# The mixer of a two-block kernel: its work ordered by the layer norm's chain, and its last four input projections as plain fp32 products

## The reference, cut to what matters

```python
p = rmsnorm(h, g) @ w_in            # 1024 -> 1792 = 14 tiles of 128 features
p_pool, p_bval, p_bgate, p_cgate, p_cx = split(p)   # 2 + 2 + 2 + 4 + 4 tiles
# a: windows of 2, 4, 8, 16 tokens: mean - u, then 64x64 products, times a scale
# b: u = v*sigmoid(gate); depthwise conv of 31 taps; layernorm over 256; silu; @ w_pw
# c: conv of 4 taps; gates r, i = sigmoid(64x64 products); a = exp(-8 r softplus(-lam));
#    h = scan(a, sqrt(1-a*a) * i * xc); times gelu(c_gate)
h = h + concat(y_a, y_b, y_c) @ w_out    # 1024 -> 1024 = 8 tiles
```

## Time and profile before

| | |
|---|---|
| median of 3 runs | 1327.17 us (1326.48 to 1327.98) |
| the profiled execution: its own time | 1329.2 us |
| its span, first to last instruction | 1327.3 us |
| mean granted TensorE clock | 0.972 |
| PE busy | 1254.1 us (94%) |
| DVE busy | 846.9 us (64%) |
| ACT busy | 598.1 us (45%) |
| POOL busy | 70.9 us (5%) |
| the mixer's input projection starts | 785.9 us |
| its output projection starts | 909.5 us |

### The profile page before, as it was taken

One profiled execution on the slowest core, in us unless ns is written; L12 is line 12 of the kernel. 1 busy time (PEld: TensorE's weight loads), 2 busy tenths in 40 slices (PEclk: granted clock), 3 DMA queues, 4 the chain that ended last, 5 costly groups with the idle time before them and its releaser, 6 DMA issues.

```text
span 1327.3 us, 17556 instructions
## 1 busy us (share of the span) xinstructions
PE 1254.1 (94%) x6213; PEld 1026.9 (77%) x6213; DVE 846.9 (64%) x1196; ACT 598.1 (45%) x909; POOL 70.9 (5%) x58
## 2 busy tenths in 40 slices
PE   7899999999979999999997899867999999999997
PEld 6688888888867887777775689865888888888885
DVE  5978888888844356666667559996655422455222
ACT  6457656676633255555555542444332211222112
POOL 0011111011100000000000000121000000000000
PEclk9999999999989999999999799979999999999998
DMA  5333233332314332222221132111333333333332
GB/s 156 108 99 112 80 112 106 100 111 79 110 33 135 95 91 69 64 79 64 63 75 36 48 95 80 55 58 48 95 88 94 95 95 91 94 94 95 110 95 79
DMA packets 203289, 115.57 MB, mean 87 GB/s; under 512 B 3456, under 2 KB 201216, under 8 KB 202224
## 3 DMA queue, kind: packets, MB, share of 16 engines
q1 hardware_dynamic: 201472, 104.50, 27.5%
q0 software_dynamic: 1776, 10.53, 2.3%
HBM read 112.85 MB, written 2.16 MB: 87 GB/s over the span
## 4 chain that ended last, share of the span: by engine, by line
PE 78%; DVE 12%; ACT 5%; issue 4%; DMA 1%; SPq 0%; DVEq 0%; POOL 0%; ACTq 0%
PE psum L508 70%; DVE arena L1784 2%; DVE arena L1635 2%; ACT w_hi L919 2%; PE psum L693 1%; DVE w_lo L1344 1%; PE psum L586 1%; PE psum L594 1%; PE psum L577 1%; PE psum L517 1%; DMA w_raw<-a_w_in 1%; ACT L1116 1%; ACT arena L1116 1%; DVE stat L1639 1%; DVE arena L1647 1%
## 5 line engine op out<-in xcount | busy, mean ns | idle before, releaser
L919 ACT ACTIVATE w_hi<-w_raw 128x1024 fp32r<-128x1024 f32 x191 | 202.1, 1058 | 513.9 <-PE psum L508 512.5
L508 PE MATMUL psum<-a_hi,w_hi 128*128 128x512 f32 (+1 forms) x1000 | 361.3, 380 | 5.9 <-DVE w_lo L1344 5.9
L508 PE MATMUL psum<-a_lo,w_hi 128*128 128x512 f32 (+1 forms) x1000 | 355.8, 374 | 0.0
L508 PE MATMUL psum<-a_hi,w_lo 128*128 128x512 f32 (+1 forms) x1000 | 353.7, 372 | 0.0
L1344 DVE TENSOR_TENSOR w_lo<-w_raw,w_hi 128x1024 fp32r<-128x1024 f32 x191 | 234.3, 1227 | 158.6 <-ACT w_hi L919 158.2
L508 PE MATMUL psum<-b_hi,w_hi 128*128 128x512 f32 x640 | 257.6, 402 | 10.0 <-DVE b_lo L1523 4.1
L508 PE MATMUL psum<-b_lo,w_hi 128*128 128x512 f32 x640 | 256.1, 400 | 0.0
L508 PE MATMUL psum<-b_hi,w_lo 128*128 128x512 f32 x640 | 254.7, 398 | 0.0
L508 PEld LDWEIGHTS psum<-a_hi,w_hi 128*128 128x128 f32 x1000 | 183.7, 191 | 43.5 <-issue 7.2
L508 PEld LDWEIGHTS psum<-a_hi,w_lo 128*128 128x128 f32 x1000 | 183.0, 191 | 33.6
L508 PEld LDWEIGHTS psum<-a_lo,w_hi 128*128 128x128 f32 x1000 | 182.9, 191 | 31.9
(11 more groups left out here) (264 smaller groups left out, 1254.5 us busy)
## 6 DMA issues: line engine op xcount, KB each, us to landing
w_raw<-a_w_in SPq DMA_DIRECT2D x49, 512.0 KB, 3.8
w_raw<-w_up SPq DMA_DIRECT2D x32, 512.0 KB, 3.9
w_raw<-w_down SPq DMA_DIRECT2D x32, 512.0 KB, 3.7
arena<-acs POOLq DMA_DIRECT2D x8, 1024.0 KB, 5.0
w_raw<-a_w_out SPq DMA_DIRECT2D x16, 512.0 KB, 3.7
w_raw<-w_kv SPq DMA_DIRECT2D x16, 512.0 KB, 3.8
w_raw<-b_w_in SPq DMA_DIRECT2D x16, 512.0 KB, 3.8
w_raw<-w_in SPq DMA_DIRECT2D x14, 512.0 KB, 3.6
```

What stands on the lines that cost most here:

```text
L508: ins = mm(out, wv[:, u.par, k, :], xv[:, k0 + k, c0:c0 + cn], start=(first and begin and i == 0 and n == 0), stop=(last and end and i == ...
L919: ac(w_hi[:, u.par, :, :], w_raw[:, u.par, :, :], ACT.Copy).then_inc(S["hi_ready"], 1)
```

## The change

The weights of units 10 to 13 (c's gates) are no longer split. ACT multiplies them in place by the norm's gain, in 8 instructions of 128x128 (`whole`), and PE multiplies them in plain fp32 with h itself, for the 512 real tokens only (`in2_gate`). Since PE then reads w_raw, SP loads a later unit into that buffer only when the product is done. The order of the three engines is rewritten around b's layer norm: all long taps lie before it, ACT applies the norm, POOL's work goes to DVE, and the output projection's first two units start with b's and a's tiles.

```diff
-        pool_sums = (pls[:, 0, :], pls[:, 1, :])
+        pool_sums = ((pls[:, 0, :], pls[:, 1, :]), (cu[:, 0, 0:POOL_PAD + T2], cu[:, 1, 0:POOL_PAD + T2]))
-        lnt = place(NT, 2 * P, at=top[0] - 8 * T2)
+        lnt = dwo.rearrange("p a b -> p (a b)").rearrange("p (a b) -> p a b", a=NT)
--- SP
             for n, c in enumerate(IN2_TILES):
+                if n >= 12:
+                    sp.wait_ge(S["unit_done"], U_IN2 + n - 1)
                 load(Lin(U_IN2 + n), t["w_in_2"], 0, Lin(c * P))
+            sp.wait_ge(S["unit_done"], U_OUT2 - 1)
+            load(Lin(U_OUT2), t["w_out_2"], 0, Lin(0))
+            sp.wait_ge(S["unit_done"], U_OUT2)
+            load(Lin(U_OUT2 + 1), t["w_out_2"], 0, Lin(P))
--- POOL
...
-                steps.mark(add(a[:, 1:n], u[:, 1:n], u[:, 0:n - 1], ALU.add))
...
-                nc.gpsimd.tensor_tensor(xc[:, j, META:T2], xc[:, j, META:T2], cg[:, j, META:T2], ALU.mult).then_inc(S["yc_ready"], 1)
--- PE
+            def in2_gate(n, ks=range(KT)):
+                u, m = Lin(U_IN2 + n), Lin(M_IN2 + n)
+                if ks[0] == 0:
+                    pe.wait_ge(S["acc_read"], (m - 1).v)
+                    pe.wait_ge(S["hi_ready"], (u + 1).v)
+                for k in ks:
+                    ins = mm(bank(2 * m.par), w_raw[:, u.par, k, :], h[:, k, META:T2],
+                             start=(k == 0), stop=(k == KT - 1), skip_group_check=True)
+                if ks[-1] == KT - 1:
+                    ins.then_inc(S["unit_done"], 1)
...
+            in2(1, ks=range(4))
...
+            for n in range(2, 7):
+                in2(n)
+            gates(0)
+            in2(7)
+            gates(1)
+            in2(8)
+            in2(9)
+            gates(2)
+            in2_gate(10)
+            gates(3)
+            in2_gate(11)
+            in2_gate(12)
+            pe.wait_ge(S["dw_ready"], 2)
...
+            ins.then_inc(S["ln_tp"], 1)
+            in2_gate(13, range(4))
             pe.wait_ge(S["ln_ready"], 1)
...
+            in2_gate(13, range(4, KT))
             pe.wait_ge(S["cs_ready"], 2)
...
+            pe.wait_ge(S["pool_ready"], 2)
...
-            pe.wait_ge(S["yl_ready"], KT + 6)
-            out2(Lin(0), (4, 5, 6, 7, 0, 1), None, True, False)
-            out2(Lin(0), (2, 3), ("yl_ready", KT + 7), False, True)
-            out2(Lin(1))
+            out2(Lin(0), (2, 3, 0, 1), ("yl_ready", KT + 1), True, False)
+            out2(Lin(1), (2, 3, 0, 1), None, True, False)
+            out2(Lin(0), (4, 5, 6, 7), ("yl_ready", KT + 5), False, True)
+            out2(Lin(1), (4, 5, 6, 7), None, False, True)
--- ACT
+            def whole(u):
+                act.wait_ge(S[f"raw{u.par}"], (u.half * 16 + 16).v)
+                for k in range(KT):
+                    ins = ac(w_raw[:, u.par, k, :], w_raw[:, u.par, k, :], ACT.Copy, scale=gfm[:, k:k + 1])
+                ins.then_inc(S["hi_ready"], 1)
...
+            ac(bnst[:, 0, 0:1], one, ACT.Sigmoid)
...
+            def first_tap_long(j):
+                act.wait_ge(S["acc_read"], M_IN2 + 2 * j + 2)
+                at = C_DWW + DW_K * j + DW_K - 1
+                ac(dwo[:, j, :], cu[:, j, DW_K - 1 + META:DW_K - 1 + T2], ACT.Identity, scale=par[:, at:at + 1],
+                   bias=par[:, C_DWB + j:C_DWB + j + 1]).then_inc(S["tap0_ready"], 1)
+            for n in range(11):
+                if n in (0, 2):
                     act.wait_ge(S["acc_read"], M_IN2 + n + 1)
                     ac(bgt, bgt, ACT.Sigmoid).then_inc(S["bg_ready"], 1)
+                if 1 <= n < 8:
+                    hi(Lin(U_IN2 + n + 2))
+                if n >= 8:
+                    whole(Lin(U_IN2 + n + 2))
+                if n in (1, 3):
+                    first_tap_long(n // 2)
+                if 4 <= n < 8:
+                    first_tap_short(n - 4)
                 if n == 8:
                     gate_roots((0, 1))
...
+            whole(Lin(U_IN2 + 13))
+            act.wait_ge(S["ln_stat"], 1)
+            root(stat_at(N_SD), bnag[:, :, 1], eps2, 1.0, S["ln_sd"])
+            act.wait_ge(S["ln_shift"], 1)
+            for i in range(NT):
+                ins = ac(lnt[:, i, :], bank(1 + 2 * (i // 2))[:, 256 * (i % 2):256 * (i % 2) + 256],
+                         ACT.Identity, scale=stat_at(N_RS + i, 1), bias=stat_at(N_R2 + i, 1))
+            ins.then_inc(S["ln_ready"], 1)
+            gate_roots((2, 3))
+            hi(Lin(U_OUT2))
...   (silu of b, gelus(0), hi(U_OUT2+1), gelus(2), b_hi of b, of a, of c)
--- DVE
+            def whole(u):
+                dve.wait_ge(S["hi_ready"], (u + 1).v)
+                nc.vector.memset(bnag[:, 0, 0:1], 0.0).then_inc(S["lo_ready"], 1)
...   (first taps dropped, scans(j0) for two j interleaved, rnn_out(j) in place of POOL's,
...    window_means() for both tiles with 8 operations, evacuate(10..13) of 512 columns)
+            TAPS = {1: 2, 2: 5, 3: 3, 4: 1, 5: 1, 6: 1, 7: 1, 8: 8, 9: 10, 10: 16}
+            for n in range(11):
+                evacuate(n)
+                if 1 <= n < 8:
+                    lo(Lin(U_IN2 + n + 2))
+                if n >= 8:
+                    whole(Lin(U_IN2 + n + 2))
...
+            evacuate(11)
+            whole(Lin(U_IN2 + 13))
+            evacuate(12)
+            layer_norm_sums()
+            one_minus_a2(2)
+            one_minus_a2(3)
+            layer_norm_shift()
+            window_means()
+            lo(Lin(U_OUT2))
+            scans(2)
+            evacuate(13)
             lo(Lin(U_OUT2 + 1))
...   (b_lo of b, b_lo of a, rnn_out(0..3), b_lo of c)
-IN2_TILES = [2, 4, 3, 5, 10, 11, 12, 13, 0, 1, 6, 7, 8, 9]
+IN2_TILES = [4, 2, 5, 3, 10, 11, 12, 13, 0, 1, 6, 7, 8, 9]
```

More of the change, by code:

```diff
@@ new lines, in _ @@
+            pe.wait_ge(S["nrs_ready"], 2)
+            spread(bank(5), stat_at(N_RS), TOKENS1, S["nrb_ready"])
+            tp(bank(7)[:, 0:META], stat[0:META, N_R2 + 4:N_R2 + 5].to_broadcast([META, P]), ident[0:META, 0:META])
+            spread(bank(4), stat_at(N_R2), TOKENS1, S["nrb_ready"])
+            in2(1, ks=range(4, KT))
+            for n in range(2, 7):
+                in2(n)
+            pe.wait_ge(S["rr_ready"], 3)
+            gates(0)
+            in2(7)
+            gates(1)
+            in2(8)
@@ new lines, in _ @@
+            in2(9)
[5 more added lines that the diff above has]
+            pe.wait_ge(S["dw_ready"], 2)
+            pe.wait_ge(S["acc_read"], M_IN2 + 10)
+            for i, (c0, cn) in enumerate(TOKENS1):
+                for j in range(2):
+                    ins = tp(bank(1 + 2 * (i // 2))[:, 256 * (i % 2) + P * j:256 * (i % 2) + P * j + P],
+                             dwo[:, j, c0:c0 + cn], ident)
+            ins.then_inc(S["ln_tp"], 1)
@@ L1791, in short_conv @@
             def short_conv(j):
-                dve.wait_ge(S["acc_read"], M_IN2 + 5 + j)
                 c = xc[:, j, :]
-                w = [par[:, C_RGW + 4 * j + k:C_RGW + 4 * j + k + 1] for k in range(4)]
-                own(ts(c, cxp[:, 3:3 + T2], w[3], par[:, C_RGB + j:C_RGB + j + 1], ALU.mult, ALU.add))
                 for k in (2, 1, 0):
@@ L1845, in layer_norm_sums @@
                 for i in range(NT):
-                    own(nc.vector.bn_stats(bnst[:, i, :], psum[:, 4 + i // 2, 256 * (i % 2):256 * (i % 2) + 256]))
+                    own(nc.vector.bn_stats(bnst[:, i, :], bank(1 + 2 * (i // 2))[:, 256 * (i % 2):256 * (i % 2) + 256]))
                 own.wait()
@@ L1892, in _ @@
                     long_tap()
+                if n == 2:
+                    gated(1)
                 if n == 8:
-                    scan(0)
-                    scan(1)
-                if n == 10:
-                    means(0)
-                if n == 11:
-                    one_minus_a2(2)
-                    one_minus_a2(3)
-                if n == 12:
-                    layer_norm_sums()
-                    scan(2)
-                    layer_norm()
-            means(1)
-            lo(Lin(U_OUT2 + 1))
-            scan(3)
+                    scans(0)
+            evacuate(11)
[9 more added lines that the diff above has]
+            evacuate(13)
+            lo(Lin(U_OUT2 + 1))
+            for j in range(2):
+                dve.wait_ge(S["yh_ready"], KT + 1 + j)
+                tt(b_lo[:, 2 + j, 0:SEQ], bank(6 + j), f32(b_hi[:, 2 + j, 0:SEQ]), ALU.subtract).then_inc(S["yl_ready"], 1)
+            for j in range(2):
+                dve.wait_ge(S["yh_ready"], KT + 3 + j)
+                stt(b_lo[:, j, 0:SEQ], bank(4 + j), par[:, C_PSC + j:C_PSC + j + 1],
+                    f32(b_hi[:, j, 0:SEQ]), ALU.mult, ALU.subtract).then_inc(S["yl_ready"], 1)
+            for j in range(4):
+                rnn_out(j)
             rnn_low(0)
             rnn_low(1)
-            for j in range(2):
-                dve.wait_ge(S["yh_ready"], KT + 5 + j)
-                stt(b_lo[:, j, 0:SEQ], bank(2 + j), par[:, C_PSC + j:C_PSC + j + 1],
-                    f32(b_hi[:, j, 0:SEQ]), ALU.mult, ALU.subtract).then_inc(S["yl_ready"], 1)
```

(3 more changed lines are left out.)

222 lines of the change are left out of this document (107 added, 115 removed).

## The result

| | before | after |
|---|---|---|
| median | 1326.83 us (1325.66 to 1327.98, 4 runs) | 1313.68 us (1309.99 to 1315.17, 4 runs) |
| ratio of the two | | 0.9897, 95% interval 0.9874 to 0.9920 |
| span of the profiled execution | 1327.3 us | 1312.7 us |
| mean granted TensorE clock | 0.972 | 0.980 |
| third output unit starts | 922.2 us | 907.9 us |

13.2 us faster by the medians; the forecast was 1313.3. The span is 14.6 us shorter, and nearly all of it lies in the mixer: up to the mixer's first square sums both profiles agree to 0.1 us, and from the third output unit to the end they take 405.1 and 404.8 us. The page of the changed kernel answers to the earlier trace rows: VectorE has 12.7 us less to do, ScalarE 12.1 more, GpSimd 17.4 less.

What follows compares the result with a forecast made beforehand. TensorE bounds the whole span, but VectorE the changed stretch. Gains of 10.5 us before the norm, 3.4 to the output projection and 1.6 of clock, less one clock loss, gave -13.9: median 1313.3 us, range 1309.5 to 1319.5.

Steps and rivals of the forecast that it cites:

- VectorE's queue sets the stretch from 845.6 on: Mixer, 845.6 to the last long tap: VectorE's operations set the time, ending at 876.3 against 886.9, 10.5 us earlier.
- last tap, first turn: End of the long taps, for which TensorE's first turn of b waits: forecast at 876.3, before at 886.9.
- plain unit on TensorE: Gate units 10 to 13 in plain fp32: 0.855 us a block, 6.84 a unit, against 5.9 for a split one.
- third unit, clock lower once: Start of the third output unit: 906.75 at full clock instead of 922.2, with one clock loss of 1.6 us taken.
- GpSimd's hindrance: VectorE's slow rows beside GpSimd's window sums: with GpSimd's compute gone, 1.7 + 3.1 + 0.5 = 5.3 us come back.
- The scaling's cost: ScalarE's eight in-place scalings from 843.2, 2.4 us, release VectorE at 845.6; its split began at 844.2, so 1.4 us lost.
- The dearer products are hidden in this order: Units 10 to 13: TensorE pays 3.8 us more in all, hidden because it waits 2.3 us for the taps.
- The order: Norm's chain from the first turn to the output projection: 19.35 us instead of 22.6, counted as 3.4 us of gain.
- The lower clock once, at the output: First two output units: a saving of 1.6 us from the lower clock was open, so the loss was taken once.
- the swing of the clock through all short waits: Second rival: the clock falls in the short waits from 856 on; gain 12 to 13 us, 1314 to 1315; chance 0.15.
- The rival of plain products at the lower level: Third rival: plain fp32 products run at 1.71 us a block, 13.7 a unit; +10 us, 1337; chance 0.03.
- rival 1: Behind the long taps: a wait replaces their 10 us; gain only 7 to 11 us, 1316 to 1320; chance 0.18.

Runs made afterwards that it cites:

- e1: The changed kernel with units 10 to 13 split into fp32r halves again instead of plain fp32 products, same order; median 1314.04 us.
- e7: The kernel before without GpSimd's six window additions, so the pool branch lacks its sums; median 1322.21 us.
- e2: The changed kernel with five additions of 128x512 on GpSimd beside the long taps; median 1317.70 us.
- e6: The kernel before with units 10 to 13 as plain fp32 products of weights scaled in place, its own order and GpSimd work kept; median 1322.76 us.
- e8: The changed kernel with four more plain products on TensorE between units 11 and 12, into a free bank; median 1317.00 us.
- e9: The changed kernel with the eight window operations moved ahead of the batch statistics, every operation kept; median 1320.35 us.
- again: The changed kernel measured and profiled again with no edit, beside the other variants on one chip; median 1312.30 us.
- e10: The kernel before with plain fp32 gate units and without GpSimd's six window additions, its own order kept; median 1319.91 us.
- e3: The changed kernel with two idle plain products on TensorE in the wait ahead of the output projection; median 1310.10 us.
- e4: The changed kernel with ScalarE's last two gelus moved behind the rounding of b's and a's tiles; median 1311.03 us.
- e5: The changed kernel with the last gelus moved late and one idle product filling the wait ahead of the output projection; median 1310.55 us.

## Why the prediction was right, step by step

**VectorE's queue sets the stretch from 845.6 on: shown.** e1 (cheaper products for TensorE, +3.0), e7 (VectorE unhindered, -4.8) and e2 (hindered, +5.1 in the taps) all move the output by about what they do to VectorE. The schedule's own marks:

| step | predicted | measured |
|---|---|---|
| eight scalings in place | 2.4 | 2.44 |
| VectorE goes on at | 845.6 | 845.8 |
| last tap, first turn | 876.3 | 876.2 |
| plain unit on TensorE | 6.84 | 13.90 for two, overlap included |
| second turn | 883.3 | 882.7 |
| b's pointwise product | 888.1 | 887.5 |
| output projection | 895.65 | 895.10 |
| third unit, clock lower once | 908.35 | 907.9 |

From the second turn on all is 0.5 us early, since VectorE takes the statistics and the shift in 3.3 us from 877.4 (880.7) and not in 3.9.

**The hit to 0.4 us is in part luck.** Four executions of the changed kernel lay between 1309.99 and 1315.17 us, and a second series gave a median of 1312.30. The sum is to be held against the marks: the third unit came 14.46 us earlier, with 13.9 forecast.

**GpSimd's hindrance: right mechanism, size off.** The sum had 5.3 us, 3.1 of it in the six taps. e7 measured 4.8 at the turn, 2.6 in the taps: four of those six wait for one another and cost 0.78 each even alone, which the sum counted for the new order and not for the old.

**The scaling's cost: counted against the wrong row.** The schedule has VectorE at the right place, 845.6, but the 1.4 us that "the change loses" there are no net loss. They are counted from the start of unit 10's split, which takes 1.15 us and is itself gone, and is in no item of what goes (three splits are, of four). By the marks the two L1809 began 0.4 us later than before. That is why the items from there on come to some 9.7 us and not to the schedule's 10.5. The schedule was right, the items were not, and the forecast of e6, made from the items, fell short of its turn.

**The dearer products are hidden in this order: shown** by e1, with 1.6 us of slack instead of 2.3 (e8); the loss comes where that ends. In the old order they are not hidden behind the turn (e6).

**The order: one piece shown, the rest argued.** The sum gave 3.4 us to the stretch between the turn and the output; by the marks it is 3.76 (22.62 before, 18.86 after). e9 shows that one piece in the wrong place there costs 6.9. The other moves, of the norm and the first taps to ScalarE and of the output's tiles, were not undone one by one.

**The lower clock once, at the output: it came so** (3.4 us at half, 1.6 lost), but no rule was behind the "once", and the experiments found none. Of the rivals, the swing of the clock through all short waits did not come: behind 2.21, 1.58 and 1.96 us of idle it stayed. A rule of the Trainium skill had spoken for it (TensorE: Matmul & The Clock Gate, A second HAM failure mode: psum-queue depth-cycling); the trace bears it out in one of four places, behind 2.18 us. The rival of plain products at the lower level falls with the 0.43 us a record. No wait took the taps' place, as rival 1 would have had it: 18.86 us lie between turn and output, and it had 22.6 and more.

## What to carry to other kernels

Where a stretch has another bound than the whole kernel, count the queue of that bound operation by operation; an exchange that costs TensorE some 4 us (6.95 against 5.9 for each of four units) and frees VectorE of four splits then pays. When listing what a change frees, count from the same row before and after. Ahead of a join, put the piece that starts the longest chain over other engines first, and keep GpSimd's two-input work away from VectorE's. Compare variants from a mark just ahead of the edit: here two profiles of one kernel agree to 0.02 us at the marks while their spans differ by 2.2. Look at the clock behind the mark all the same.

## What the runs showed of the hardware that was not expected

- Five additions of 128x512 on GpSimd, 1.26 us each where VectorE hardly hindered them, took 5.1 us out of VectorE's two-input operations (e2), and a 0.17 us operation took 1.1 us longer beside one (e7).
- The length of a wait alone does not say whether the clock falls. Ahead of the output projection it fell behind 2.15 to 2.19 us in the changed order (after, again, e1, e2, e8) and behind 2.20 in e9, but not behind 2.26 us in e6 and e10. With waits of 0.47 to 1.70 us it never fell there. Ahead of the gates of tile 2 it stayed behind 2.20 to 2.22 us in the changed kernel and in e2, e3, e4, e5, e8 and e9, and fell behind 1.82 us in e7. What else decides stays open.
- The same work ahead of the mark reached its end between 781.6 and 789.3 us from one execution to the next; the granted clock in its stretches differed.
